# The head sums of squares of a recurrent mixer: one full-precision matmul replaced by two rounded-format ones, placed inside the next projection

## The reference

```
o = oc.transpose(1, 0, 3, 2, 4).reshape(b, s, HGRN_HEADS, HGRN_V)
o = o * lax.rsqrt(jnp.mean(o * o, axis=-1, keepdims=True) + NORM_EPS)
o = o * norm_gain.astype(jnp.float32).reshape(HGRN_HEADS, HGRN_V)
o = o.reshape(b, s, HGRN_WIDTH) * jax.nn.silu(gate.astype(jnp.float32))
```

## Time and profile before

| what | us |
|---|---|
| median of 3 runs | 1962.08 |
| lowest, highest | 1962.07, 1962.19 |
| the profiled execution, its own time | 1962.52 |
| its span, first to last instruction | 1960.5 |

### The profile page before, as it was taken

One profiled execution on the slowest core, in us unless ns is written; L12 is line 12 of the kernel. 1 busy time (PEld: TensorE's weight loads), 2 busy tenths in 40 slices (PEclk: granted clock), 3 DMA queues, 4 the chain that ended last, 5 costly groups with the idle time before them and its releaser, 6 DMA issues.

```text
span 1960.5 us, 29474 instructions
## 1 busy us (share of the span) xinstructions
PE 1921.4 (98%) x11282; PEld 1581.3 (81%) x11282; DVE 693.7 (35%) x1103; ACT 694.3 (35%) x1034; POOL 871.4 (44%) x407
## 2 busy tenths in 40 slices
PE   6999999999999999999999999999999999999997
PEld 5888888877778788888888888888777788888887
DVE  4322210276566422210162222104666672222103
ACT  4332322354545332322252323224554452323221
POOL 5444444462325544445363434445432254434452
PEclk9999999999999999999999999999999999999999
DMA  5323232331112222223223222322311123222331
GB/s 171 104 94 101 92 108 97 108 108 56 57 53 86 99 94 98 94 97 114 102 79 104 91 101 92 111 97 87 108 66 55 55 86 107 90 102 92 102 109 63
DMA packets 54041, 182.82 MB, mean 93 GB/s; under 512 B 6696, under 2 KB 10312, under 8 KB 53960
## 3 DMA queue, kind: packets, MB, share of 16 engines
q1 hardware_dynamic: 53960, 181.65, 27.3%
HBM read 179.14 MB, written 2.49 MB: 93 GB/s over the span
## 4 chain that ended last, share of the span: by engine, by line
PE 91%; DVE 5%; issue 1%; POOL 1%; DVEq 1%; POOLq 1%; DMA 0%; ACT 0%; SPq 0%; ACTq 0%
PE bank L732 26%; PE bank L734 25%; PE bank L733 25%; PE pair L897 2%; DVE HLO L1107 2%; PE bank L758 2%; PE bank L750 2%; PE bank L751 2%; PE pair L732 1%; PE pair L734 1%; PE pair L733 1%; DVE SM L1261 1%; POOL WLO L375 1%; PE pair L776 1%; DVE X L1097 1%
## 5 line engine op out<-in xcount | busy, mean ns | idle before, releaser
L375 POOL TENSOR_TENSOR WLO<-RAW,WHI 128x1024 fp32r<-128x1024 f32 (+1 forms) x336 | 795.6, 2387 | 1033.8 <-ACT WHI L445 861.8
L733 PE MATMUL bank<-HLO,WHI 128*128 128x512 f32 (+1 forms) x1632 | 632.3, 387 | 0.0
L732 PE MATMUL bank<-HHI,WHI 128*128 128x512 f32 x1568 | 620.6, 396 | 1.5 <-DVE TMP L1056 1.0
L734 PE MATMUL bank<-HHI,WLO 128*128 128x512 f32 x1568 | 610.9, 390 | 0.0
L445 ACT ACTIVATE WHI<-RAW 128x1024 fp32r<-128x1024 f32 (+1 forms) x336 | 337.4, 1038 | 82.3 <-PE bank L734 61.5
L733 PEld LDWEIGHTS bank<-HLO,WHI 128*128 128x128 f32 x1632 | 306.6, 188 | 60.6 <-issue 0.5
L732 PEld LDWEIGHTS bank<-HHI,WHI 128*128 128x128 f32 x1568 | 294.3, 188 | 67.6 <-issue 3.2
L734 PEld LDWEIGHTS bank<-HHI,WLO 128*128 128x128 f32 x1568 | 294.4, 188 | 62.1
L732 PE MATMUL bank<-UHI,WHI 128*128 128x512 f32 x616 | 242.7, 394 | 0.0
L734 PE MATMUL bank<-UHI,WLO 128*128 128x512 f32 x616 | 241.5, 392 | 0.0
L733 PE MATMUL bank<-ULO,WHI 128*128 128x512 f32 x616 | 239.0, 388 | 0.0
(11 more groups left out here) (196 smaller groups left out, 1824.9 us busy)
## 6 DMA issues: line engine op xcount, KB each, us to landing
RAW<-stream SPq DMA_DIRECT2D x336, 512.0 KB, 3.7
X<-xT SPq DMA_DIRECT2D x4, 512.0 KB, 8.9
yT<-X SPq DMA_DIRECT2D x16, 128.0 KB, 1.8
bias<-rel_scratch SPq DMA_DIRECT2D x4, 128.0 KB
rel_scratch<-SM SPq DMA_DIRECT2D x1, 382.0 KB
mask_sb<-masks SPq DMA_DIRECT2D x1, 256.0 KB, 10.5
par<-sinks SPq DMA_DIRECT2D x4, 2.0 KB, 4.2
par<-params SPq DMA_DIRECT2D x1, 60.0 KB, 2.3
```

Source lines behind the costliest of these rows:

```text
L375: pool.tensor_tensor(WLO[:, n, 0:cols], RAW[:, n, 0:cols], WHI[:, n, 0:cols], ALU.subtract)\
L732: pe.matmul(dst, WHI[:, slot, lhs], rhs_hi, start=first, stop=False)
L733: pe.matmul(dst, WHI[:, slot, lhs], rhs_lo, start=False, stop=False)
L734: ins = pe.matmul(dst, WLO[:, slot, lhs], rhs_hi, start=False, stop=last)
```

## The change

The square of the recurrent output is split in two float32r parts. ACT squares to YSQ, drains, and copies YSQ to YSQH, and signals `yh_sq` only then; the copy to Y comes third. DVE subtracts YSQH from YSQ into YSQL (`square_low`) and signals `yh_sq_lo`. PE multiplies both parts by a float32r `block_ones_r`. In the loop the pair of matmuls is placed after the fifth k-tile of `next_group(0)` and writes bank 3; the closing one stays where it was, in bank 7. `head_norm` moves behind the exponentials on ACT, PE's wait for `yh_r` moves from `scores(0)` to behind `scores(4)`, and POOL's wait for `logit_ready` becomes one for `yh_sq_lo` in rounds 1 to 3.

```
-                        total(YSQ[:], 7, (yh_sq, it), yh_sum, block_ones)
...
-                    next_group(0)
+                    if t == 0:
+                        next_group(0)
+                    else:
+                        next_group(0, 0, 5)
+                        head_total(it, 3)
+                        next_group(0, 5, KT)
...
+            def head_total(n, b):
+
+                pe.wait_ge(block_ready, 1)
+                pe.wait_ge(yh_sq, n)
+                pe.matmul(bank[b][:], block_ones_r[:], YSQH[:], start=True, stop=False)
+                pe.wait_ge(yh_sq_lo, n)
+                pe.matmul(bank[b][:], block_ones_r[:], YSQL[:], start=False, stop=True).then_inc(yh_sum, 1)
...
-                            pe.wait_ge(yh_r, it + 1)
...
                     scores(4)
+                    pe.wait_ge(yh_r, it + 1)
...
-                total(YSQ[:], 7, (yh_sq, L * NT + NT), yh_sum, block_ones)
+                head_total(L * NT + NT, 7)
...
-                    act.activation(YSQ[:], bank[6][:], ACT.Square).then_inc(yh_sq, 1)
+                    act.activation(YSQ[:], bank[6][:], ACT.Square)
+                    act.drain()
+                    act.activation(YSQH[:], YSQ[:], ACT.Copy).then_inc(yh_sq, 1)
                     act.activation(Y[:, NT + t, :], bank[6][:], ACT.Copy).then_inc(yh_read, 1)
...
+                    def square_low(n):
+
+                        dve.wait_ge(yh_sq, n)
+                        dve.tensor_tensor(YSQL[:], YSQ[:], YSQH[:], ALU.subtract).then_inc(yh_sq_lo, 1)
...
                     dve.tensor_tensor(paired(Ssink), paired(top), sink, ALU.subtract).then_inc(logit_ready, 1)
+                    if t > 0:
+                        square_low(it)
...
                     next_take(3)
+                    if t == NT - 1:
+                        square_low(it + 1)
...
-                    pool.wait_ge(logit_ready, it + 1)
+                    if t == 0:
+                        pool.wait_ge(logit_ready, it + 1)
+                    else:
+                        pool.wait_ge(yh_sq_lo, it)
...
             dve.wait_ge(const_ready, 1)
+            dve.tensor_copy(block_ones_r[:], block_ones[:]).then_inc(block_ready, 1)
```

More of the change, by code:

```diff
@@ L189, in build_program @@
         block_ones = sb("block_ones", [P, P])
+        block_ones_r = sb("block_ones_r", [P, P], F32R)
         ident = sb("ident", [P, P])
@@ L219, in build_program @@
         YSQ = sb("YSQ", [P, SEQ])
+        YSQH = sb("YSQH", [P, SEQ], F32R)
+        YSQL = sb("YSQL", [P, SEQ], F32R)
         RP = sb("RP", [P, SEQ])
@@ L293, in build_program @@
         yh_sum = sem("yh_sum")
+        yh_sq_lo = sem("yh_sq_lo")
+        block_ready = sem("block_ready")
         yh_read = sem("yh_read")
@@ L618, in head_norm @@
                     act.wait_ge(yh_sum, L * NT + (t + 1))
-                    rsqrt_mean(YR[:, t, :], bank[7][:], HEAD_DIM).then_inc(yh_r, 1)
+                    rsqrt_mean(YR[:, t, :], bank[7 if t == NT - 1 else 3][:], HEAD_DIM).then_inc(yh_r, 1)
                 for c in range(C_GROUP0 + 2, C_GROUPS):
@@ L651, in mixer @@
                     act.activation(VTOK[:].rearrange("p a b -> p (a b)"), bank[6][:], ACT.Copy).then_inc(vtok_ready, 1)
-                    if t > 0:
-                        head_norm(t - 1)
                     act.wait_ge(logit_ready, it + 1)
@@ L658, in mixer @@
                     act.activation(Ssink, Ssink, ACT.Exp).then_inc(exp_ready, 1)
+                    if t > 0:
+                        head_norm(t - 1)
                     for half in range(2):
```

## The result

The changed kernel takes 1965.57 us (median of 20 runs, 1965.40 to 1965.76), the kernel before 1962.13 (median of 20, 1961.91 to 1962.29): ratio 1.0018, 95% interval 1.0011 to 1.0024. That is 3.4 us or 0.18% more, where 3.0 were forecast (1965.1, range 1961.3 to 1967.6); it lies in the outcome with the largest chance, within 0.2% of the kernel before, though the interval is clear of no change.

The account below looks back on a forecast made before the run. PE was taken to bound the kernel, busy 1921.4 of 1960.5 us. Six loop places at 0.18 + 0.46 = 0.64 us (+3.8) and the closing places (-0.8) gave +3.0 us, 1965.1 us, range 1961.3 to 1967.6.

Parts of the forecast that it names:

- the outcome with the largest chance: Whole kernel: time within 0.2% (3.9 us) of the kernel before, chance 0.67.
- The wait that takes the removed sum's place: Loop, PE's transposes: a wait for ACT's copy to Y replaces the sum's 0.97 us; projection starts 0.18 us later.
- The pair: Loop, projection behind the fifth k-tile: two added matmuls at 0.228 us each cost 0.46 us a place.
- The closing places: Output projection: sum's 0.86 us replaced by the pair's 0.47, gaining 0.39 twice, -0.8 us; DVE's late scaling stays hidden.
- The cover: Closing place, tile 4: ZHI ready at 575.9, wanted by PE at 577.3, 1.4 us of slack.
- Nothing absorbs the shift: Rest of each round: DVE's clock runs from PE's, so PE's shift goes through to the round's end.
- The low part and the moved steps: Loop: subtraction ends 0.8 us before PE needs it; moved norm, POOL's split and ACT's steps cost nothing.
- The sum: Whole kernel: +3.8 us in the loop and -0.8 us in the closing places give +3.0 us, 1965.1 us.
- The rival with a cheap step on ACT: Loop, transposes: PE's wait ends as early as before, -0.05 a place, 1961.0 us; chance 0.15 with space to forecast.
- The gain for all of the removed time: Loop, transposes: gap closes, each place gains 0.51 us and closing ones 0.39, -3.9 us, 1958.2; chance 0.03.
- The late low part: Behind the fifth k-tile: POOL's split holds the subtraction, PE waits 1.6 us in six places, 1975 us; chance 0.05.
- the overrun closing chain: `out_high(4)` or later tile: PE waits about 1 us twice, 1967.1 us; chance 0.15 together with dearer drain.

Follow-up runs that it names:

- e1_swap: Changed kernel with ACT's copy of bank 6 to Y straight behind the square, ahead of the drain and the copy to YSQH; 1961.34 us.
- e7_two_copies: Changed kernel with ACT making the copy to YSQH twice, a drain between, before the copy to Y, in all eight places; 1971.56 us.
- e6_pool_old_wait: Changed kernel with POOL's wait in rounds 1 to 3 put back to `logit_ready`; 1965.70 us.
- e8_closing_delay: Changed kernel with five useless DVE subtractions behind the closing subtraction of each layer, ahead of the scaling of the recurrent outputs; 1972.17 us.
- e3_late_transposes: As e1_swap, with the four transposes of column I behind the second k-tile of the projection in rounds 1 to 3; 1959.19 us.
- e5_closing_alone: Kernel before with only the fourth round's square split in high and low parts and the pair in the output projection; 1961.28 us.

## Why the prediction was right, point by point

**The wait that takes the removed sum's place.** Right, and the main step: e1_swap and e7_two_copies move this wait alone, down and up, and the time follows. From the square's start to the first projection matmul it was 2.07 us before, was forecast at 2.25, and came out at 2.31 in five places and 2.59 in one. Two pieces were off in opposite directions: PE starts 0.15 us after the copy to Y ends (459.57, 459.72), not the 0.06 I took from the earlier trace rows, and the transposes take 0.38 us to the first projection matmul, not 0.42. ACT's part was right to 0.01 us: the copy to Y ended 1.78 us after the square's start, forecast 1.77. The one longer place has 0.35 us ahead of L703 that ended on nothing that the profile shows:

```profile
533.41 0.63 ACT L703 ACTIVATE YSQH<-YSQ 128x512 fp32r<-128x512 f32 x1 [0.35 <-issue]
```

e6_pool_old_wait and e8_closing_delay show the same 0.35 in the same place, e7_two_copies in the other layer, e1_swap and e3_late_transposes none. What it is stays open.

**The pair.** Forecast 0.46, measured 464.07 - 463.60 = 0.47. A place thus costs 0.24 + 0.47 = 0.71 where 0.64 was forecast; six places are 4.3, with the one delay 4.5, where 3.8 was forecast.

**The closing places.** Forecast -0.8; measured alone -0.87 (e5_closing_alone). DVE's scaling started late as forecast; the block by POOL hit the first step of the second tile (L1206 at 575.09) instead of the second step of the first one, which changed nothing on PE. The cover came out at 1.7 us where 1.4 were forecast, but by another path: the forecast had tile 4 wait for DVE, and it waited for ACT's table load (to 577.31), a step that the prediction does not have.

**Nothing absorbs the shift.** Nearly right. The rounds grew by 0.71, 0.61 and 0.99 us in layer 0 and by 0.70, 0.61 and 0.65 in layer 1, from square to square. That is 4.3 in all, where the places alone, with the 0.28 of the longer one, give 4.5: about 0.2 is given back later in the rounds.

**The low part and the moved steps.** Right: PE shows no wait at L794, the exponentials did not move, and the norm and POOL's split are out of the way. The subtraction ran from 461.93 to 462.61. ACT's weight split moved by 0.7 us (from 458.67 to 459.47, less the 0.09 by which the whole round is later), where at most 0.5 was forecast, and PE shows no wait for it.

**The sum.** The rounds give +4.3 and the rest of the two layers -0.9, which is the 3.4 of the medians (the profiled spans differ by 3.5). The forecast of +3.0 was low by the 0.07 us in each of six places and by the one delay, 0.7 in all, and the part given back in the rounds took some 0.2 off that again; the nearness of 3.0 to 3.4 owes something to this.

**The rivals.** The rival with a cheap step on ACT fell with the 1.10 us wait, and e1_swap shows what it would have given: 1961.34, where 1961.0 was forecast. The gain for all of the removed time was excluded rightly: even the best order keeps 0.41 us of wait in the old place. The late low part and the overrun closing chain did not occur. What no rival had is the clock: in two places of the experiments a wait of 2.1 us cost more than its own length.

## What to carry to other kernels

Before taking an instruction out of a full engine's queue, look at what the next instruction there waits for and when that comes: here 0.97 us of matmul stood in front of transposes that could start only 0.5 us earlier without it, and the step added on ACT to make the cheaper format put them 0.7 us later. An added step on a helper engine goes behind the step that somebody waits for (4.2 us here, two lines exchanged). Then the cheaper format pays its 0.42 us in each place. Last, give the full engine independent work across the wait that is left, here another 2.1 us.

## What the runs showed of the hardware that was not expected

The granted clock of PE fell after waits of 2.08 and 2.13 us in two profiled places (0.59 and 0.63 in the stretches behind them, matmuls 0.43 us apart for eight starts), and not after every such wait: in e7_two_copies the other five places waited 1.79 to 1.80 us, and the matmuls behind them started 0.23 apart at once, as they did in layer 1 of e8_closing_delay behind a wait of 2.14 us. Behind the changed kernel's waits of 1.10 us the clock was 1.00. So an idle time of 2 us here sometimes costs 1.5 us beyond itself, and its length alone does not decide, since 2.08 us had the fall and 2.14 us had not. The longest of the four runs of e8_closing_delay, 1973.50 us, has a mean granted clock of 0.996 where the other three, 1971.88 to 1972.43, have 0.998; one more such fall would fit, but this run was not profiled. What decides when was not tested.
